# The down tiles' pair loads are issued from ScalarE's queue from the fifth expert on

## Chip, cores and metric

The kernel runs on one core of one Trainium2 chip. The metric is the device time of one execution in microseconds. Three runs of the kernel before give a median of 1706.59 us (1705.27 to 1707.78).

## The reference, cut to what matters

The program computes a two-layer transformer block and then a second block that ends in a mixture of experts. All weights are float32 and are read once. The change touches only the loads of the experts' weights:

```python
def expert_choice_ffn(h, w_router, w_gate, w_up, w_down):   # 16 experts
    cap = 2 * L // 16                                       # L = 272 tokens, cap = 34
    ...
    g, idx = lax.top_k(aff.T, cap)
    xg = hs[idx]                                            # 34 tokens of an expert
    a = jnp.einsum('ecd,edf->ecf', xg, w_gate)              # 1024 x 2048
    u = jnp.einsum('ecd,edf->ecf', xg, w_up)                # 1024 x 2048
    y = jnp.einsum('ecf,efd->ecd', jax.nn.silu(a) * u, w_down)   # 2048 x 1024
    ...
```

One expert needs 24 MB of weights (8 MB each for gate, up and down) and works on only 34 tokens.

## The kernel before

The kernel is one hand-written program for each engine, held together by semaphores. Weights come through a ring of six slots of 2 MB in SBUF (`RING_T`); the list `LOADS` fixes which tile goes into which slot and in which order. The experts' weights are cut into tiles of 2 MB: g0 to g3, u0 to u3 and d0 to d3 for each expert. From the fifth expert on (`PAIR_FROM = 4`, counting from zero) two neighbouring tiles make one pair of 4 MB that is loaded by one DMA into two neighbouring slots. An expert is then six pairs, in this order: G0, G1, G2, G3 (each gate tile with its up tile) and D0, D1 (d0 with d1, d2 with d3). Six slots are three pairs, so pair n goes where pair n-3 was: D0 of an expert follows G1 of the same expert, D1 follows G2, and G0, G1, G2 and G3 of the next expert follow G3, D0, D1 and that expert's own G0. The experts 4 to 14 are loaded this way whole; the last one, 15, has G0 to G2 as pairs and the rest in tiles and pieces.

SyncE issues every DMA (`sync_program`). For a pair, `pair_ring` (L3402 to L3408) waits at L3405 and L3406 until both slots have been left and issues the DMA at L3408. A slot is left when TensorE's last matmul that reads it is done: for a G pair this is the semaphore `u.full` of its PSUM bank, for a down tile `edown` or the bank of the expert's output.

TensorE (`pe_experts`) goes through an expert in this order: `gate_up(e, 0)`; in experts 3, 5, 7, 9, 11, 13 and 14 a `combine` of earlier outputs; `gate_up(e, 1)` to `gate_up(e, 3)`, each followed by the transposes of the hidden tile before it (`turn_hidden`, L1424); `down(e, 0)`; the gather of the next expert's tokens (`pick`, L1370); `down(e, 1)` to `down(e, 3)` with the transposes of `turn_picks` before the last. `gate_up` is the matmuls of L1412 and L1413, `down` those of L1439 and L1440.

ScalarE (`act_experts`) runs `gate(e, i)` for each gate tile: it waits for `u.full` of `gate_up(e, i)` and for VectorE's use of the buffer two tiles back, then one Silu (L2159). At the end of an expert it evicts two of the picks and one half of the output (L2184). VectorE multiplies (L3095), copies the transposed tiles and evicts the other half (L3136).

Of the kernel before, what the change touches and what calls it, by code (L numbers as in the profile page):

```python
# [24 lines left out]
E_N = 16  # L25
# [84 lines left out]
PAIR_FROM = 4  # L110
# [170 lines left out]
def flat(a):  # L281
    return a.rearrange("p a b -> p (a b)")
# [1239 lines left out]
def act_table(nc, n):  # L1522
    nc.scalar.add_instruction(mybir.InstLoadActFuncSet(
        name=nc.get_next_instruction_name(), engine=mybir.EngineType.Activation, act_func_set_id=n, ins=[], outs=[]))


def act_out(nc, u, dst, src, f=ACT.Copy, **kw):

    nc.scalar.wait_ge(u.full, u.n)
    nc.scalar.activation(dst, src, f, **kw).then_inc(u.taken, 1)  # L1530


def act_rms(nc, k, name, ps, n, a):

    i, s, u = RMS_AT[name], k.sem, k.banks["rms", name]
    nc.scalar.wait_ge(u.full, u.n)
    nc.scalar.activation(a, ps, ACT.Ln, bias=k.cc("eps"), scale=1.0 / n).then_inc(s["ln"], 1)
    nc.scalar.wait_ge(s["ln"], 2 * i + 1)
    nc.scalar.activation(a, a, ACT.Exp, scale=-0.5).then_inc(s["ln"], 1)
# [587 lines left out]
def act_experts(nc, k):  # L2127
    act, s, v, P = nc.scalar, k.sem, k.ex, k.banks
    act_out(nc, P["router"], v.LG, P["router"].t[:, 0:L])
    act_rms(nc, k, "ffn2", P["rms", "ffn2"].t[:, 0:3], D, v.RQ[:, 2, :])  # L2130
    u, roots = P["route"], v.RQ[:, 0, :]
    act.wait_ge(u.full, u.n)
    act.wait_ge(s["rscaled"], 1)
    for i, (r, m) in enumerate(TILES):
        act.activation(v.AFF[0:m, i, :], u.v(3, 16)[0:m, i, :], ACT.Exp, bias=v.mx[0:m, i:i + 1], scale=roots[0:m, i:i + 1],
                       accum_out=v.sm[0:m, i:i + 1]).then_inc(s["rexp"] if i < 2 else u.taken, 1)

    def turn_tokens(i):
        m = TILES[i][1]
        for half in range(2):  # L2140
            act_out(nc, P["tokens", i, half], v.FT[0:m, i, half * 512:half * 512 + 512], P["tokens", i, half].t[0:m, :],
                    scale=roots[0:m, i:i + 1])

    for i in range(3):
        turn_tokens(i)
    act_out(nc, P["affinity"], v.WK[0:16, 6:6 + L], P["affinity"].t[0:16, 0:L])

    def pick(e):
        for half in range(2):
            u = P["picks", e, half]  # L2150
            act_out(nc, u, v.XT[0:CAP, 256 * half:256 * half + 256], u.t[0:CAP, 0:256])

    def gate(e, i):
        u = P["egu", e, i]
        act.wait_ge(u.full, u.n)
        if 4 * e + i >= 2:
            t = P["egu", e, i - 2] if i >= 2 else P["egu", e - 1, i + 2]
            act.wait_ge(t.taken, t.done)
        act.activation(v.SG[:, i % 2, :], u.t[0:CAP, :], ACT.Silu).then_inc(s["esilu"], 1)  # L2159

    act_table(nc, SET_SILU)
    pick(0)
    for e in range(E_N):
        gate(e, 0)
        if 1 <= e <= 8:
            act_out(nc, P["back", e - 1], v.OGT[0:NP, e - 1, :], P["back", e - 1].t[0:NP, 0:L])
        for i in range(1, 4):
            gate(e, i)
        if e < E_N - 1:
            for q in range(4):  # L2170
                t = P["turned", e, q]
                act.wait_ge(t.full, t.n)
            pick(e + 1)
        else:
            act_table(nc, SET_EXP)

        u, g, r = P["eo", e], e // 2, 64 * (e % 2)
        act.wait_ge(u.full, u.n)
        if e == 0:
            act.wait_ge(s["yzero"], 1)  # L2180
        if g >= 2:
            t = P["comb", g - 2, KC - 1]
            act.wait_ge(t.full, t.n)
        act.activation(v.Y[r:r + CAP, g % 2, 0:512], u.t[0:CAP, :], ACT.Copy).then_inc(u.taken, 1)  # L2184

    def squares(i, half):
        u, n = P["fin", i, half], 2 * i + half
        act.wait_ge(u.full, u.n)
        act.activation(k.HWC[:, 512 * n:512 * n + 512], u.t[:, :], ACT.Square, accum_out=v.ss[:, i, half:half + 1]).then_inc(u.taken, 1)

    def root(i):
        a = v.fr[:, i, 1:2]
        act.wait_ge(s["fin_rs"], 5 * i + 1)
        act.activation(a, v.fr[:, i, 0:1], ACT.Ln, bias=k.cc("eps"), scale=1.0 / D).then_inc(s["fin_root"], 1)
        act.wait_ge(s["fin_root"], 2 * i + 1)
        act.activation(a, a, ACT.Exp, scale=-0.5).then_inc(s["fin_root"], 1)

    def final(i):
        x = v.XF[:, i, 512:1024]
        act.wait_ge(s["weighed"], 2 * i + 2)  # L2200
        act.wait_ge(s["fin_rs"], 5 * i + 5)
        act.activation(x, x, ACT.Identity, scale=v.fr[:, i, 3:4]).then_inc(s["final_a"], 1)

    squares(0, 0)
    squares(0, 1)
    squares(1, 0)
    root(0)
    squares(1, 1)
    root(1)
    final(0)  # L2210
    final(1)


def scalar_program(nc, k):
    high, split = [ActHigh(nc, k, layer) for layer in range(2)], ActSplit(nc, k)
    act_ab(nc, k, high[0])
    act_ffn(nc, k, 0, high[0], split)
    act_cd(nc, k, high[1])
    act_ffn(nc, k, 1, high[1], split)
    act_diff(nc, k, split)  # L2220
    act_experts(nc, k)
# [1073 lines left out]
def sync_program(nc, k):  # L3295
    sp, s, A, P = nc.sync, k.sem, k.A, k.banks
# [49 lines left out]
    u = P["rms", "mix1"]  # L3346
# [8 lines left out]
    def part(x, e, i):  # L3355

        if x == "d":
            return A["w_down_2"][e, i // 2][:, SLOT * (i % 2):SLOT * (i % 2 + 1)]
        return A["w_gate_up_2"][e, i][:, SLOT * (x == "u"):SLOT * (x == "u") + SLOT]
# [20 lines left out]
    u = P["rms", "ffn2"]  # L3380
# [15 lines left out]
    def beside_ring(x, e, i):  # L3396

        w = k.weight_at(x, e, i)
        sp.wait_ge(*w.prev.left)
        sp.dma_start(w.t, part(x, e, i)).then_inc(w.sem, 16)  # L3400

    def pair_ring(x, e, i):  # L3402

        head, tail = k.ring[x, e, i], k.ring[("u", e, i) if x == "g" else ("d", e, i + 1)]
        sp.wait_ge(*head.prev.left)  # L3405
        sp.wait_ge(*tail.prev.left)  # L3406
        src = A["w_gate_up_2"][e, i] if x == "g" else A["w_down_2"][e, i // 2]
        sp.dma_start(flat(k.ring.pair((x, e, i))), src).then_inc(head.sem, 16)  # L3408

    heads = set(PAIRED.values())  # L3410
    for e in range(E_N):
        if e:
            for i in range(4):
                for x in "gu":
                    if (x, e, i) in heads:
                        pair_ring(x, e, i)
                    elif (x, e, i) in PAIRED:
                        continue
                    elif (x, e, i) not in PIECES_OF and (x, e, i) != ("u", E_N - 1, 3):
                        beside_ring(x, e, i)  # L3420
        if e == 5:

            sp.wait_ge(*k.first["g", 3, 0].left)
            sp.dma_start(k.CB[:, :], A["fin"].broadcast_to([128, D])).then_inc(s["fin_in"], 16)
        if e == E_N - 1:


            w = k.ring["u", e, 3]
            sp.wait_ge(*w.prev.left)
            for c in range(2):  # L3430
                a, b = 2 * D * c, 2 * D * (c + 1)
                sp.dma_start(w.t[:, a:b], part("u", e, 3)[:, a:b]).then_inc(s[f"lastu{c}"], 16)
        for i in range(4):
            if ("d", e, i) in heads:
                pair_ring("d", e, i)
            elif e and (e < E_N - 1 or i < 2) and ("d", e, i) not in PIECES_OF and ("d", e, i) not in PAIRED:
                beside_ring("d", e, i)
    for i, n, first in ((2, 2, 0), (3, 4, 2)):
# [12 lines left out]
def build(nc, A, out):  # L3451
    k = Kit(nc, A, out)
    tensor_program(nc, k)
    scalar_program(nc, k)
    vector_program(nc, k)
    gpsimd_program(nc, k)
    sync_program(nc, k)
# [112 lines left out]
```

## Time and profile before

| | |
|---|---|
| median of three runs | 1706.59 us |
| the profiled execution, its own time | 1706.8 us |
| its span in the profile | 1704.9 us |
| TensorE busy | 1598.6 us, 94% |
| DMA bytes, mean rate over the span | 577.69 MB, 339 GB/s |
| pairs of 4 MB issued (G and D) | 47 and 22 |

How to read it: times in a trace are microseconds from the start of the span, and some 2 us of an execution lie outside it. TensorE (PE in the rows) is counted as busy while a matmul is in flight, even in stretches in which it waits for weights between tiles, so its 94% doesn't say that it is the bound. SPq is SyncE's own instruction stream, where a DMA shows only the time that issuing takes; the transfer itself shows as the time from issue to landing. A row "A <-B" with a time names who ended the idle time of A.

### The profile page before, as it was taken

What the parts mean: (1) busy time and instruction counts of PE and PEld (TensorE: products, weight loads), DVE (VectorE), ACT (ScalarE), POOL (GpSimd) and SP (SyncE); (2) the same over time, 40 slices, a digit from 0 to 9 for tenths busy, and PEclk for the clock granted to TensorE, in tenths of its full rate; (3) what the DMA queues carried; (4) which work ended last, traced back from release to release, by engine and by line L of the source; (5) the groups of instructions that cost most, each with busy time, mean ns of one, the idle gap of its engine ahead of it and who ended that gap; (6) DMA issues with size and microseconds to landing.
All of it is one profiled execution on the core that took longest, in us unless ns stands there. A gap on an engine that the chain in (4) does not pass through costs nothing.

```text
span 1704.9 us, 22910 instructions
## 1 busy us (share of the span) xinstructions
PE 1598.6 (94%) x9593; PEld 978.8 (57%) x9593; DVE 734.6 (43%) x1462; ACT 472.4 (28%) x839; POOL 34.3 (2%) x39
## 2 busy tenths in 40 slices
PE   7999999999999999999999989889889888888898
PEld 5787999998999999787322322323223223223332
DVE  3778889888886557895111111101101101011111
ACT  2526644448653437743000000000000000000001
POOL 0101000000000000100100000000000000000000
PEclk9999999999999999999999999999999999999999
DMA  9855478892466554249999999999999999999997
GB/s 388 354 244 216 170 314 343 324 353 84 173 254 223 190 195 176 100 155 391 402 429 430 431 435 433 432 433 431 431 433 433 434 431 431 431 434 432 431 430 297
DMA packets 36964, 577.69 MB, mean 339 GB/s; under 512 B 4192, under 2 KB 5248, under 8 KB 8192
## 3 DMA queue, kind: packets, MB, share of 16 engines
q1 hardware_dynamic: 36864, 576.24, 81.6%
q8 instruction: 77, 1.26, 0.3%
q14 instruction: 23, 0.19, 0.0%
HBM read 575.17 MB, written 1.05 MB: 338 GB/s over the span
## 4 chain that ended last, share of the span: by engine, by line
PE 70%; DMA 25%; DVE 2%; issue 2%; ACT 1%; SPq 0%; DVEq 0%; ACTq 0%
DMA RING_T<-in_w_gate_up 24%; PE P L1412 16%; PE P L1439 7%; PE P L986 5%; PE P L988 5%; PE P L987 5%; PE P L590 4%; PE P L1004 2%; PE P L1003 2%; PE P L1005 2%; PE P L599 2%; PE P L1370 1%; DMA RING_T<-in_w_down 1%; PE P L1174 1%; PE P L1176 1%
## 5 line engine op out<-in xcount | busy, mean ns | idle before, releaser
L1412 PE MATMUL P<-RING_T,SCR 128*34 128x512 f32 x928 | 421.5, 608 | 64.7 <-DMA RING_T<-in_w_gate_up 59.8
L1413 PE MATMUL P<-RING_T,SCR 128*34 128x512 f32 x960 | 436.7, 609 | 0.0
L1412 PEld LDWEIGHTS P<-RING_T,SCR 128*34 128x34 f32 x928 | 101.2, 114 | 332.3 <-issue 311.8
L3095 DVE TENSOR_TENSOR SCR<-P,SCR 34x512 f32<-34x512 f32 x64 | 44.4, 693 | 495.8 <-ACT SCR L2159 495.7
L1439 PE MATMUL P<-RING_T,SCR 128*34 128x512 f32 x480 | 220.6, 608 | 20.4 <-issue 19.6
L1440 PE MATMUL P<-RING_T,SCR 128*34 128x512 f32 x480 | 220.8, 609 | 0.0
L2159 ACT ACTIVATE SCR<-P 34x512 f32<-34x512 f32 x64 | 37.7, 589 | 538.1 <-PE P L1413 538.1
L986 PE MATMUL P<-SCF 128*128 128x256 f32 x640 | 181.1, 283 | 0.0
L988 PE MATMUL P<-SCF 128*128 128x256 f32 x640 | 181.1, 283 | 0.0
L987 PE MATMUL P<-SCF 128*128 128x256 f32 x640 | 181.1, 283 | 0.0
L1439 PEld LDWEIGHTS P<-RING_T,SCR 128*34 128x34 f32 x480 | 51.0, 114 | 153.5 <-issue 149.3
L986 PEld LDWEIGHTS P<-SCF 128*128 128x128 f32 x640 | 122.9, 192 | 0.0
L988 PEld LDWEIGHTS P<-SCF 128*128 128x128 f32 x640 | 122.9, 192 | 0.0
L987 PEld LDWEIGHTS P<-SCF 128*128 128x128 f32 x640 | 122.9, 192 | 0.0
L2644 DVE TENSOR_TENSOR SCF<-RING_T,SCF 128x1024 fp32r<-128x1024 f32 x88 | 106.1, 1220 | 30.0 <-ACT SCF L1808 30.0
L1808 ACT ACTIVATE SCF<-RING_T 128x1024 fp32r<-128x1024 f32 x88 | 91.9, 1053 | 52.7 <-PE P L1005 27.9
L1413 PEld LDWEIGHTS P<-RING_T,SCR 128*34 128x34 f32 x960 | 104.7, 114 | 0.0
L1530 ACT ACTIVATE SCR<-P 128x256 f32<-128x256 f32 (+7 forms) x112 | 45.1, 417 | 197.4 <-PE P L1370 122.8
L1003 PE MATMUL P<-SCF 128*128 128x256 f32 x352 | 99.6, 283 | 0.0
L1004 PE MATMUL P<-SCF 128*128 128x256 f32 x352 | 99.6, 283 | 0.0
L1005 PE MATMUL P<-SCF 128*128 128x256 f32 x352 | 99.6, 283 | 0.0
L2317 DVE SCALAR_TENSOR_TENSOR RING_T<-RING_T,CB 128x1024 f32<-128x1024 f32 x80 | 94.2, 1232 | 8.0 <-ACT CB L1623 4.1
(465 smaller groups left out, 2529.9 us busy)
## 6 DMA issues: line engine op xcount, KB each, us to landing
RING_T<-in_w_gate_up SPq DMA_DIRECT2D x47, 4096.0 KB, 20.7
RING_T<-in_w_down SPq DMA_DIRECT2D x22, 4096.0 KB, 21.7
RING_T<-in_ada_w SPq DMA_DIRECT2D x24, 2048.0 KB, 10.6
RING_T<-in_ffn_w SPq DMA_DIRECT2D x22, 2048.0 KB, 8.0
RING_T<-in_w_gate_up SPq DMA_DIRECT2D x17, 2048.0 KB, 16.8
RING_T<-in_ffn_w SPq DMA_DIRECT2D x22, 1024.0 KB, 6.6
RING_T<-in_w_down SPq DMA_DIRECT2D x11, 2048.0 KB, 17.6
RING_T<-in_ab_w_in SPq DMA_DIRECT2D x7, 2048.0 KB, 15.8
```

What stands on the lines that cost most here:

```text
L986: pe.matmul(o, wh, v.HH[:, 0, c, :], start=c == 0, stop=False)
L987: pe.matmul(o, wh, v.HH[:, 1, c, :], start=False, stop=False)
L988: ins = pe.matmul(o, wl, v.HH[:, 0, c, :], start=False, stop=c == KC - 1)
L1003: pe.matmul(o, wh, v.HR[:, f % NHD, 0, :], start=f == 0 and m % 2 == 0, stop=False, skip_group_check=True)
L1004: pe.matmul(o, wh, v.HR[:, f % NHD, 1, :], start=False, stop=False, skip_group_check=True)
L1005: ins = pe.matmul(o, wl, v.HR[:, f % NHD, 0, :], start=False, stop=f == 21, skip_group_check=True)
L1412: pe.matmul(u.t[0:CAP, :], xs, wg.v(KC, 512)[:, c, :], start=c == 0, stop=c == KC - 1)
L1413: ins = pe.matmul(u.t[64:64 + CAP, :], xs, wu.v(KC, 512)[:, c, :], start=c == 0, stop=c == KC - 1)
L1439: pe.matmul(u.t[0:CAP, :], hs, w.v(4, 1024)[:, c, 0:512], start=first, stop=end)
L1440: ins = pe.matmul(u.t[64:64 + CAP, :], hs, w.v(4, 1024)[:, c, 512:1024], start=first, stop=end)
L2317: nc.vector.scalar_tensor_tensor(out=src, in0=src, scalar=1.0, in1=k.CB[:, :], op0=ALU.mult, op1=ALU.mult, accum_out=k.MOD[:, layer, 4 * i ...
L2644: nc.vector.tensor_tensor(lo, w.up()[:, :, z, j * 128:(j + 1) * 128], hi.bitcast(F32), ALU.subtract).then_inc(k.sem["lo"], 1)
```

## The change

The DMAs that load D0 and D1 of experts 4 to 14 (22 DMAs of 4 MB) are taken out of SyncE's program and put into ScalarE's, behind `gate(e, 1)` and `gate(e, 2)`. Their waits, their sources, the slots that they fill and the semaphores that they raise stay the same. The G pairs, the last expert's loads and all else stay in SyncE's program in their order.

```diff
@@ act_experts @@
+    def load_downs(e, i):
+
+        head, tail = k.ring["d", e, i], k.ring["d", e, i + 1]
+        act.wait_ge(*head.prev.left)
+        act.wait_ge(*tail.prev.left)
+        act.dma_start(flat(k.ring.pair(("d", e, i))), k.A["w_down_2"][e, i // 2]).then_inc(head.sem, 16)
+
...
         for i in range(1, 4):
             gate(e, i)
+            if PAIR_FROM <= e < E_N - 1 and i < 3:
+                load_downs(e, 2 * (i - 1))
@@ sync_program @@
-    def pair_ring(x, e, i):
-
-        head, tail = k.ring[x, e, i], k.ring[("u", e, i) if x == "g" else ("d", e, i + 1)]
+    def pair_ring(e, i):
+
+        head, tail = k.ring["g", e, i], k.ring["u", e, i]
         sp.wait_ge(*head.prev.left)
         sp.wait_ge(*tail.prev.left)
-        src = A["w_gate_up_2"][e, i] if x == "g" else A["w_down_2"][e, i // 2]
-        sp.dma_start(flat(k.ring.pair((x, e, i))), src).then_inc(head.sem, 16)
+        sp.dma_start(flat(k.ring.pair(("g", e, i))), A["w_gate_up_2"][e, i]).then_inc(head.sem, 16)
...
             if ("d", e, i) in heads:
-                pair_ring("d", e, i)
+                continue
```

## Rows read from the trace of the kernel before

**Rows 1.** The page: DMA's share and rate in 40 slices; queues with packets, MB, share.

```profile
DMA  9855478892466554249999999999999999999997
GB/s 388 354 244 216 170 314 343 324 353 84 173 254 223 190 195 176 100 155 391 402 429 430 431 435 433 432 433 431 431 433 433 434 431 431 431 434 432 431 430 297
q1 hardware_dynamic: 36864, 576.24, 81.6%
```

**Rows 2.** Busy time by stretch: PE, PEld, DVE, ACT, POOL, then granted clock, DMA share, GB/s.

```profile
1416.50:1474.40 57.90, 52.57 (x258) 17.65 (x256) 9.11 (x23) 3.70 (x7) 0.00 (x0) 0.97 1.00 431
1474.40:1532.30 57.90, 48.71 (x242) 15.12 (x240) 6.15 (x15) 3.70 (x7) 0.00 (x0) 0.97 1.01 434
```

**Rows 3.** Waits from 1000 us on: engine, line, releaser, us in total, times, longest.

```profile
ACT SCR L2159 <- PE P L1413: 422.7, 48, 11.4
PE P L1412 <- DMA RING_T<-in_w_gate_up: 59.8, 35, 3.0
```

**Rows 4.** PE in order of time: four tiles' first matmuls, and the kernel's last weights.

```profile
1478.55 0.59 PE L1412 MATMUL P<-RING_T,SCR 128*34 128x512 f32 x1 [1.66 <-DMA RING_T<-in_w_gate_up]
...
1488.28 0.59 PE L1412 MATMUL P<-RING_T,SCR 128*34 128x512 f32 x1 [2.30 <-DMA RING_T<-in_w_gate_up]
...
1497.94 0.59 PE L1412 MATMUL P<-RING_T,SCR 128*34 128x512 f32 x1 [2.24 <-DMA RING_T<-in_w_gate_up]
...
1507.56 1.04 PE L1439 MATMUL P<-RING_T,SCR 128*34 128x512 f32 x1 [2.19 <-issue]
...
1693.21 0.62 PE L1439 MATMUL P<-RING_T,SCR 128*34 128x512 f32 x1 [0.16 <-DMA RING_T<-in_w_down]
```

**Rows 5.** SyncE in order of time: the six issues of expert 12, and the next.

```profile
1447.00 0.33 SPq L3408 DMA_DIRECT2D RING_T<-in_w_gate_up  x1
...
1461.76 0.33 SPq L3408 DMA_DIRECT2D RING_T<-in_w_gate_up  x1
...
1469.12 0.33 SPq L3408 DMA_DIRECT2D RING_T<-in_w_gate_up  x1
...
1476.98 0.33 SPq L3408 DMA_DIRECT2D RING_T<-in_w_gate_up  x1
...
1485.69 0.33 SPq L3408 DMA_DIRECT2D RING_T<-in_w_down  x1
...
1495.42 0.33 SPq L3408 DMA_DIRECT2D RING_T<-in_w_down  x1
...
1505.08 0.33 SPq L3408 DMA_DIRECT2D RING_T<-in_w_gate_up  x1
```

**Rows 6.** One issue of L3408 by itself: duration in ns, and its landing.

```profile
L3408 SPq DMA_DIRECT2D RING_T<-in_w_down x1: 328/328/328, 1485.7 to 1485.7; - x1
DMA to landing us min/median/max: 21.8/21.8/21.8
```

**Rows 7.** DMA issues of the whole kernel: count, KB each, median us to landing.

```profile
RING_T<-in_w_down SPq DMA_DIRECT2D x22, 4096.0 KB, 21.7
out<-SCR SPq DMA_DIRECT2D x4, 256.0 KB, 2.0
```

**Rows 8.** ACT in order of time: two Silus of expert 12.

```profile
1485.65 0.59 ACT L2159 ACTIVATE SCR<-P 34x512 f32<-34x512 f32 x1 [8.12 <-PE P L1413]
1495.38 0.59 ACT L2159 ACTIVATE SCR<-P 34x512 f32<-34x512 f32 x1 [9.14 <-PE P L1413]
```

**Rows 9.** PE in order of time: D0's start, the next G0's start, a combine.

```profile
1449.49 1.04 PE L1439 MATMUL P<-RING_T,SCR 128*34 128x512 f32 x1 [2.21 <-issue]
...
1469.83 0.62 PE L1412 MATMUL P<-RING_T,SCR 128*34 128x512 f32 x1 [0.80 <-DVE SCR L3136]
...
1534.86 3.94 PE L1455 MATMUL P<-SCR 98*128 98x272 f32 x16
```

**Rows 10.** The chain of waits: two loads from issue to landing; the instruction queue, 1300 to 1323.

```profile
1271.33 21.83 DMA RING_T<-in_w_gate_up
1300.55 22.34 DMA RING_T<-in_w_gate_up
...
q8 instruction: 1, 0.02, 0.2%
```

More of the change, by code:

```diff
@@ L3415, in sync_program @@
                     if (x, e, i) in heads:
-                        pair_ring(x, e, i)
+                        pair_ring(e, i)
                     elif (x, e, i) in PAIRED:
```

## The prediction

> **What bounds the kernel now.** I read the page's slices first. From the slice that starts at 853 us (20 x 42.6) the 16 DMA engines are busy all the time and move 429 to 435 GB/s, until the last slice [rows 1]; nearly everything goes through one queue, q1, which is SyncE's. Then busy time by stretch, in the part with pairs: DMA share 1.00 and 1.01, while TensorE's clock is at 0.97 and ScalarE is busy for 3.70 of 57.9 us [rows 2]. Then the waits: over the stage TensorE waits 59.8 us for gate and up weights in 35 waits, and ScalarE waits for TensorE [rows 3]. Then four tiles in order of time: each first matmul starts when its weights land, at 1478.55, 1488.28, 1497.94 and 1507.56, so a pair takes (1507.56 - 1478.55) / 3 = 9.67 us; the last wait is booked as "issue", but D0 was issued at 1485.69 and landed 21.8 us later, at 1507.5, so it is weights too [rows 4, 5, 6]. 4 MB in 9.67 us is 434 GB/s. An expert of six pairs is 58.0 us. The last matmuls still wait for weights at 1693.21 [rows 4]. So the end of the kernel is set by one stream of bytes that never pauses. What counts for a change is one thing: does it make that stream pause, or move faster.
>
> **What the queue looks like inside.** Of three pairs of slots one is being read by TensorE, one is on the wire, and one is queued. D0 is issued at 1485.69, when G1 has been read, and lands 21.8 us later; its own transfer is 9.67, so for 12.1 us it waits, behind 2.5 us of G2's rest and 9.67 of G3. G1's reading takes 1485.69 - 1478.55 = 7.1 us of the 9.67 [rows 4, 5, 6].
>
> **Part 1: 22 DMAs leave SyncE.** There are 22 [rows 7], at 0.33 us of issuing each [rows 5]. SyncE issues each G pair as soon as its slots are free and waits between (from 1485.69 to 1495.42 it has one thing to do) [rows 5], so this frees nothing: G0 to G3 wait for their own slots, which come free at the same times. 0 us.
>
> **Part 2: ScalarE issues them.** D0 goes behind gate(e, 1), which waits for the same matmul that leaves D0's slots, so the added waits pass at once. ScalarE's Silu of G1 starts at 1485.65, 0.04 us before SyncE's issue of D0, and takes 0.59 [rows 5, 8]. The issue is thus between 0 and 0.6 us later; I take 0.6. Queued behind it on ScalarE is gate(e, 2), 9.7 us away [rows 8], for which 0.33 us of issuing is nothing; VectorE and the transposes that wait for the Silu see no difference. That cover would be gone only if ScalarE were held at a wait, and none that the change adds can hold it. 0 us by itself, since the byte stream has 12.1 us of queue ahead of D0.
>
> **Part 3: two queues instead of one.** This is the only part with a price. In one queue D0 can't overtake G3. In two it can, and no row of this kernel shows two load queues at once. I take it that the engines serve both alike, since the small instruction packets of q8 get through while q1 is 20 us deep [rows 10]. Then the bytes in flight are the same, but G3 lands late. By hand for one expert, zero at G1's landing, steps of 9.67: G1 is read by 7.3, D0 is issued at 7.9. The shortest transfer in the trace lands 2.0 us after its issue, and its 256 KB are 0.6 of them, so 1.4 us pass until bytes flow [rows 7]: D0 moves from 9.3. G2 lands at about 9.9. Then G3 and D0 share, and both land near 29.0, where before G3 landed at 19.3 and D0 at 29.0. TensorE reads G2 until 17.2 (D1 is issued and queues behind D0), stands idle, and reads G3 from 29.1 to 36.3, or 37.9 if it restarts at half clock (D0's first matmul takes 1.04 us after a wait, others 0.59, some 1.6 us over the tile) [rows 4]. D1 has the wire alone from 29.0 and would land at 38.7. The next G0 is issued when G3 has been read, and its bytes come at 37.7 to 39.3: the stream pauses for 0 to 0.6 us. Then TensorE goes from G3 to D0 (1.0 us), and D0's slots come free 12.3 us after D0's start, 10.7 without the half clock (1449.49 to 1461.76) [rows 5, 9]: the next G1 is issued near 48.0 to 49.6, its bytes come at 49.4 to 51.0, and G0's bytes end at 48.4. A pause of 1.0 to 2.6 us. After that D1's slots are free 7.4 us later (1461.76 to 1469.12) [rows 5] and there is no further pause. Sum for the first expert with two queues: 1.0 to 3.2 us.
>
> The second expert is milder, because TensorE is now behind: it reads its G1 some 4 us later against the landing, so D0 is issued later, meets a G3 that is 3.6 us into its transfer, and G3 lands 6.1 us late, not 9.7. G0's bytes then come 4.7 us before the wire would run dry, and G1's 2.6 us before. In an expert with a combine (5, 7, 9, 11, 13, 14) another 3.94 us [rows 9] push D0's issue further back, and G3 is 2.1 us late. TensorE needs some 51 us for an expert without its waits (50.4 by the steps 7.1 x 4, three gaps of about 0.9 and 1469.83 - 1449.49 less 1.6), and 55 with a combine, of 58.0 [rows 4, 9]: it can make up what it lost. The other quiet experts (6, 8, 10, 12) come out between a pause of 0 and one like the first. I take 1.4 for the first, 0.2 for each of the four others, 0 for the six with a combine: +2.2 us. Bounds of this part: 0 (TensorE's lag always covers) and 5 x 3.2 = 16 (every quiet expert pays in full).
>
> **Sum.** The profiled execution took 1706.8 us, its span of 1704.9 and 1.9 around it: 1706.8 + 2.2 = 1709.0. It stands 0.2 above the median of the three runs, so I forecast 1708.8. The 11.7 us behind the last weights (1693.21 to 1704.9) [rows 4] stay as they are, since the last expert is in one queue again.
>
> **A rule of the skill.** The Trainium skill, "DMA: Bandwidth & Descriptors", section "Issuing engines are not separate DMA queues", says that DMAs of all issuers end on the same 16 engines and interleave, and that several issuers save only the issuing time; by it this change could gain nothing. The stream here is never short of issued work [rows 1, 2], which agrees. The same page, section "Queues, rings and completion order", says that an engine takes turns between queues and changes over only when a whole packet is done, where a packet is some 9 to 17 descriptors. By it an engine's share of a pair could be one packet, and the pairs would alternate whole; the time for that is rival 1.
>
> **Rival 1: whole pairs take turns.** D0 then goes on the wire as soon as G2 is done, at 9.7, and G3 behind it: D0 lands at 19.3, G3 at 29.0. G3 is as late as in the fair case, in each quiet expert, for a G3 that has already queued doesn't profit from TensorE's lag unless it has begun. For it: D0 is issued before G2 is done [rows 5, 6]. Against it: nothing in the rows. It pays about 0.6 us in each of the 11 experts, 1 us in the quiet ones: 6 to 8 us, 1714. Chance 0.17.
>
> **Rival 2: changing queues costs wire time.** The nearest rows: two loads in a row that land at 1293.16 and 1322.89, three steps apart, 29.73 and not 29.01 us, with one instruction packet of 16 KB between [rows 10]. At 27 GB/s an engine that packet is 0.6 us; 0.12 is over, for going there and back. If a pair is eight pieces per engine and each change costs 0.06 us, an expert with 16 to 30 changes loses 1 to 1.8 us: 11 to 20 us over 11 experts, 1722. It decides as soon as a change costs over 0.02 us. Chance 0.07.
>
> **Rival 3: one queue starves the other.** If ScalarE's queue always went first, D0 and D1 (issued at 17.8, before D0 is through) would both go ahead of G3: it lands at 38.7 with nothing left in flight, and the wire stands still until G3 is read and G0's bytes come, 7.2 + 0.1 + 1.4 = 8.7 us. Over 11 experts 96 us, some 1803. For it speaks only that no row shows the order; against it that q8 gets through. Chance 0.05.
>
> **Rival 4: the stream gets denser.** The best slice has 435 GB/s, the others of the stage 429 to 434, 432 in the mean [rows 1]. If a second queue fills the seams between DMAs and all slices come to 435, 0.7% of some 620 us are gained: 4.3 us, 1702.3. For it: the room exists. Against: the queue is never empty, and the pair's step of 9.67 is already 434. Chance 0.09.
>
> **Rival 5: the change does nothing.** If the engines kept the order of issue, all would stay at 1706.6. Chance 0.10.
>
> **How the numbers follow.** The fair case has 0.52. A measurement of this kernel can tell about 0.2% from no change, 3.4 us. The fair case lies within that for most of its range and reaches past it with about 0.05; rival 5 lies within; rival 1 is past it, with about 0.03 within. Faster 0.09 (rival 4); same 0.52 - 0.05 + 0.10 + 0.03 = 0.60; slower 0.05 + 0.14 + 0.07 + 0.05 = 0.31. The range of 1703.5 to 1719 leaves out most of rival 4, the upper half of rival 2 and rival 3, some 0.17.
>
> **What would show it.** DMA share in the stretches stays 1.00 and the rate 431 to 434; q1 splits, with 22 x 4 MB (92 MB) in a second queue. D0's time to landing stays near 21, or gets shorter, G3's grows from about 21 to 25 to 30 us. TensorE's waits for G3 get longer (3.0 is the longest now) and those for D0 and G0 go away; the sum of its waits stays. Rate under 425 in the stage would speak for rival 2; stretches with DMA share under 0.9 once per expert for rival 3. I am wrong if the stage gets shorter, or if pauses add up to more than 3 us.

## The result, and the profile after

The changed kernel took 1721.6 us, 1719.0 and 1723.9 us in three executions; a fourth took 4088 us and is left out (with it the median is 1722.74). Against 1706.57 us before, the ratio is 1.009, with an interval of 1.0076 to 1.0104: 15 us slower. I had forecast 1708.8 us and a range up to 1719.0. The profiled execution took 1721.58 us, its span grew from 1704.9 to 1719.6, by 14.7 us.

The page of the kernel after: rate in 40 slices, queues (packets, MB, share of 16 engines), and the issues of pairs (count, KB, median us to landing).

```profile
GB/s 390 355 245 202 185 305 363 320 346 56 208 237 241 151 241 146 126 172 377 406 430 430 434 432 397 427 424 429 426 417 417 428 414 425 432 403 436 429 431 305
q1 hardware_dynamic: 33696, 483.96, 68.9%
q10 hardware_dynamic: 3168, 92.28, 12.5%
RING_T<-in_w_gate_up SPq DMA_DIRECT2D x47, 4096.0 KB, 16.6
RING_T<-in_w_down ACTq DMA_DIRECT2D x22, 4096.0 KB, 21.4
```

The 22 DMAs moved as the diff says: 92 MB now go through q10. The stage that ran at 429 to 435 GB/s [rows 1] has slices of 397, 403, 414 and 417. The next fence is busy time by stretch of the kernel after (us, PE, PEld, DVE, ACT and POOL busy, granted clock, DMA share, GB/s): one stretch in which two pairs share the wire, then the pauses: two behind the late G3 of expert 4, one behind the late D1 of expert 5 (1127 to 1133), one in expert 6 (1177 to 1183), and two each behind the late G3 of the experts 8, 10 and 12.

```profile
1264.00:1280.00 16.00, 6.98 (x32) 2.37 (x30) 0.99 (x2) 0.59 (x1) 0.00 (x0) 0.71 1.02 440
...
1045.00:1051.00 6.00, 6.00 (x34) 1.77 (x32) 0.99 (x2) 0.59 (x1) 0.00 (x0) 1.00 0.68 240
1057.00:1063.00 6.00, 6.00 (x36) 1.78 (x34) 0.27 (x2) 0.00 (x0) 0.00 (x0) 1.00 0.91 344
1127.00:1133.00 6.00, 5.20 (x26) 1.32 (x24) 0.69 (x1) 0.59 (x1) 0.00 (x0) 1.00 1.01 399
1177.00:1183.00 6.00, 6.00 (x38) 1.73 (x34) 0.64 (x4) 0.00 (x0) 0.00 (x0) 1.00 0.93 377
1286.00:1292.00 6.00, 6.00 (x34) 1.83 (x30) 0.99 (x2) 0.59 (x1) 0.00 (x0) 1.00 0.71 268
1298.00:1304.00 6.00, 6.00 (x36) 1.78 (x34) 0.64 (x4) 0.00 (x0) 0.00 (x0) 1.00 0.91 350
1405.00:1411.00 6.00, 6.00 (x32) 1.69 (x28) 0.99 (x2) 0.59 (x1) 0.00 (x0) 1.00 0.77 279
1417.00:1423.00 6.00, 6.00 (x36) 1.72 (x34) 0.64 (x4) 0.00 (x0) 0.00 (x0) 1.00 0.92 350
1525.00:1531.00 6.00, 6.00 (x35) 1.82 (x32) 0.99 (x2) 0.59 (x1) 0.00 (x0) 1.00 0.84 317
1536.00:1542.00 6.00, 6.00 (x36) 1.78 (x34) 0.63 (x4) 0.00 (x0) 0.00 (x0) 1.00 0.91 350
```

While both queues are served the rate is 440 GB/s, not less than with one (435 in the same stretch before). The loss is in pauses. Against 432 GB/s, 6 us at 268 are 6 x (1 - 268/432) = 2.3 us, at 350 another 1.1: expert 8 pays 3.4 us. By the same sum expert 4 pays 3.9, expert 10 3.3, expert 12 2.7, expert 6 0.8, and expert 5, which has a combine, 0.5: 14.5 us, where the span grew by 14.7. The landings of G1 say the same of the experts without a combine: from their G1 to the next expert's pass 62.0, 59.5, 60.9, 61.8 and 61.2 us, where before they were 58.1 to 58.2, together 14.6 us more. That these sums meet the 14.7 to 0.2 us is partly chance: the executions of the changed kernel lie 4.9 us apart, and in the trace of before the same stretch takes 59.5 us in the experts 9 and 13, which in the change have 58.0 and 58.1.

One expert in detail, expert 8. Its gate and up pairs on SyncE and its down pairs on ScalarE, in order of time (start, duration), and the first matmul of G3:

```profile
1251.33 0.33 SPq L3416 DMA_DIRECT2D RING_T<-in_w_gate_up  x1
...
1258.79 0.59 ACT L2159 ACTIVATE SCR<-P 34x512 f32<-34x512 f32 x1 [6.48 <-PE P L1413]
1258.85 0.33 ACTq L2166 DMA_DIRECT2D RING_T<-in_w_down  x1
...
1279.37 1.04 PE L1412 MATMUL P<-RING_T,SCR 128*34 128x512 f32 x1 [9.02 <-DMA RING_T<-in_w_gate_up]
...
1287.93 0.33 SPq L3416 DMA_DIRECT2D RING_T<-in_w_gate_up  x1
...
1298.87 0.33 SPq L3416 DMA_DIRECT2D RING_T<-in_w_gate_up  x1
```

The times to landing of four of these issues by themselves: G3 (issued at 1251.33), D0 (1258.85), D1 (1270.08), the next G0 (1287.93).

```profile
DMA to landing us min/median/max: 27.9/27.9/27.9
...
DMA to landing us min/median/max: 21.6/21.6/21.6
...
DMA to landing us min/median/max: 20.6/20.6/20.6
...
DMA to landing us min/median/max: 12.4/12.4/12.4
```

G3 lands at 1279.2 and D0 at 1280.5, together: they shared the wire. The two queues by themselves, from 1264 to 1274 (packets, MB, share of 16 engines), and the stretch in which TensorE starts on G3:

```profile
q10 hardware_dynamic: 70, 2.29, 53.1%
q1 hardware_dynamic: 71, 2.13, 49.3%
...
1279.30:1281.30 2.00, 1.94 (x6) 0.66 (x8) 0.00 (x0) 0.00 (x0) 0.00 (x0) 0.50 0.95 410
```

ScalarE's queue (q10) and SyncE's (q1) move about the same. TensorE stood idle for 9.0 us ahead of G3 and started it at a granted clock of 0.50, the lower of its two levels (1.2 of 2.4 GHz), with 1.04 us a matmul, not 0.59. It released G3 at 1287.9; D1 lands at 1290.7, and the next G0, issued on a wire about to run dry, takes 12.4 us, where its bytes need 9.67. ScalarE is innocent of lateness: its issue stands 0.06 us behind the start of its Silu.

### The profile page after: what moved, and what is told of

Read it like the earlier page. It is cut to its first block, busy times and chain, and to the rows that moved or that the text cites. A ratio compares the mean times of both kernels' runs of the same rounds, so it can differ in the third digit from the quotient of the medians.

```text
span 1719.6 us, 22910 instructions
## 1 busy us (share of the span) xinstructions
PE 1603.2 (93%) x9593; PEld 970.5 (56%) x9593; DVE 735.3 (43%) x1462; ACT 472.9 (27%) x839; POOL 34.3 (2%) x39
## 3 DMA queue, kind: packets, MB, share of 16 engines
q10 hardware_dynamic: 3168, 92.28, 12.5%
## 4 chain that ended last, share of the span: by engine, by line
PE 78%; DMA 17%; DVE 2%; ACT 1%; issue 1%; SPq 0%; DVEq 0%; ACTq 0%
PE P L1412 19%; DMA RING_T<-in_w_gate_up 13%; PE P L1439 11%; PE P L986 4%; PE P L988 4%; PE P L987 4%; DMA RING_T<-in_w_down 4%; PE P L590 4%; PE P L1004 2%; PE P L1003 2%; PE P L1005 2%; PE P L1370 2%; PE P L599 2%; PE P L1174 1%; PE P L1175 1%; PE P L1176 1%
## 6 DMA issues: line engine op xcount, KB each, us to landing
RING_T<-in_w_gate_up SPq DMA_DIRECT2D x17, 2048.0 KB, 14.8
```

## Experiments

Theory P at the start: the pauses behind an overtaken G3 are the whole loss, and only experts without a combine have them. Rival S: a second queue costs wire time by itself. Rival L: ScalarE issues late.

### Half of the experts

```diff
+ON_ACT = (4, 6, 8, 10, 12)            # second kernel: (5, 7, 9, 11, 13, 14)
-            if PAIR_FROM <= e < E_N - 1 and i < 3:
+            if e in ON_ACT and i < 3:
```

> The down pairs of experts 4, 6, 8, 10 and 12 alone (those without a combine) are issued from ScalarE's queue, the others stay in SyncE's. Theory P (pauses): D0 overtakes G3, and the stream runs dry twice behind a late G3, only in experts without a combine, where each costs 3.1 us. The whole loss of the change, 15 to 16 us, is then here: 1721 to 1724 us. Rival S (a second queue costs wire time whenever it is in use, 16 us over 11 experts, 1.45 each): 5 x 1.45 = 7 us, 1714 us.

> The down pairs of experts 5, 7, 9, 11, 13 and 14 alone (those with a combine) are issued from ScalarE's queue. Theory P: D0 is issued some 4 us later against the stream there, G3 is already on the wire, and nothing runs dry: 0 to 3 us, 1707 to 1710 us (expert 14 follows another with a combine and has the least certain place). Rival S: 6 x 1.45 = 9 us, 1715 us.

Measured, as the ratio to the kernel before with its interval: 1.0087 (1.0069 to 1.0106), 14.8 us, for the experts without a combine; 1.0067 (1.0043 to 1.0092), 11.4 us, for the others. The first is what P said. The second fits neither. The two halves together lose 26 us where the whole change loses 15, so the cost isn't one per use of the queue, which speaks against S, and it isn't tied to the missing combine either, which speaks against P: an expert with a combine is spared in the full change only because of what the expert before it has left behind. The traces bear this out: in expert 9 D0 is issued 12.7 us after G1's landing in the change and 8.6 us when only the experts with a combine are changed, and G3 then takes 28.9 us to land, not 21.2.

### Later issues

```diff
-            if PAIR_FROM <= e < E_N - 1 and i < 3:
-                load_downs(e, 2 * (i - 1))
+            if PAIR_FROM <= e < E_N - 1 and i > 1:      # one tile later
+                load_downs(e, 2 * (i - 2))
...
+                for _ in range(5):                      # other kernel: 3 us of dependent copies ahead of load_downs
+                    ...
+                    act.activation(v.LG[:, 0:256], k.C[:, 0:256], ACT.Copy).then_inc(s["delay"], 1)
```

> As the change, but D0 is issued behind gate(e, 2) and D1 behind gate(e, 3), one gate tile later each. Theory P: D0's bytes come some 19 us after G1's landing, when G3 is through or nearly so, so nothing overtakes: 1706 to 1709 us, though both queues are in use. Rival S: unchanged, 22 pairs still use the second queue, 1720 to 1724 us.

> As the change, but five dependent copies on ScalarE, about 3 us together, stand ahead of each of the 22 issues. Theory P: G3 has 3 us more on the wire before D0 joins, lands 3 us earlier, and the pauses of 2 and 1 us in a quiet expert are mostly covered: 1707 to 1711 us; issuing later makes it faster. Rival L (the loss comes from ScalarE issuing late or being held up): slower than the change, 1724 us or more. Rival S: as the change, 1720 to 1724 us.

Measured: 1.0576 (1.0551 to 1.06), 98 us slower, and 1.0143 (1.0121 to 1.0165), 24 us slower. P falls as I had put it. The second time, 1732 us, is what rival L forecast (1724 or more), so L is left to the next experiment. The trace of the later issues shows what I had left out: D1 and the next expert's G0, issued at the same moment, and their times to landing.

```profile
1238.55 0.33 SPq L3416 DMA_DIRECT2D RING_T<-in_w_gate_up  x1
1238.56 0.36 ACTq L2166 DMA_DIRECT2D RING_T<-in_w_down  x1
...
DMA to landing us min/median/max: 25.4/25.4/25.4
...
DMA to landing us min/median/max: 23.0/23.0/23.0
```

The first landing is D1's, the second G0's. TensorE needs D1 before G0, but they share the wire all the way, and D1 comes last. Two of this kernel's dry stretches:

```profile
1202.00:1208.00 6.00, 5.21 (x26) 1.30 (x24) 0.69 (x1) 0.59 (x1) 0.00 (x0) 1.00 0.56 193
1225.00:1234.00 9.00, 9.00 (x48) 2.53 (x45) 1.39 (x4) 0.59 (x1) 0.00 (x0) 1.00 0.22 65
```

So there can be two crossings in an expert, D0 with G3 and D1 with the next G0, and a later issue relieves the first and feeds the second. Theory Q, from here on: what costs is any pair that shares the wire with one that TensorE needs earlier.

### One queue again, but ScalarE's

```diff
+        load_gates(e, 3)               # behind gate(e, 0)
...
+        load_gates(e + 1, 0)           # behind gate(e, 3)
+            load_gates(e + 1, 1)       # behind pick(e + 1)
+        load_gates(e + 1, 2)           # behind the eviction of the expert's output
-                        pair_ring(e, i)
+                        if e == PAIR_FROM:
+                            pair_ring(e, i)
```

> From expert 5's G0 on every pair, G and D, is issued from ScalarE's queue in the old order, so the stream is in one queue again (only around experts 4 and 15 both are in use). Theory Q (order): what costs is that with two queues a pair shares the wire with one that TensorE needs earlier (D0 with G3, the next G0 with D1). In one queue none does: 1706 to 1711 us. Rival A (ScalarE as the issuer costs: late issues, a slower queue): 1722 us or more, with 67 issues instead of 22.

Measured: 1.0032 (1.0021 to 1.0043), 5.5 us slower, a median of 1711.57 us, just past Q's figure. Two stretches of it, the border at expert 4, where its D0 is in one queue and its G3 in the other, and 520 us of the stage:

```profile
1045.00:1062.00 17.00, 17.00 (x97) 5.02 (x94) 2.15 (x5) 1.34 (x3) 0.00 (x0) 1.00 0.94 371
1070.00:1590.00 520.00, 457.62 (x2244) 151.45 (x2242) 71.04 (x175) 34.91 (x67) 0.00 (x0) 0.97 1.00 433
```

17 x (1 - 371/432) = 2.4 us are lost at this crossing; then 433 GB/s for the rest of the stage, against 423 in the change. ScalarE issues 65 pairs here and the stage loses no rate by it, so L is out. The rest of the 5.5 us lies at the other border, in expert 15, whose G2 comes from ScalarE's queue and the tiles behind it from SyncE's: G2 takes 24.7 us to land, where before it took 20.5, TensorE waits 4.5 us for it, and the span ends 16.5 us behind the last weights, not 11.7.

### One of the two pairs

```diff
-            if PAIR_FROM <= e < E_N - 1 and i < 3:
+            if PAIR_FROM <= e < E_N - 1 and i == 1:     # D0 alone; other kernel: i == 2, D1 alone
```

> As the change, but only D0 is issued from ScalarE's queue; D1 goes back to SyncE's, behind G3 and ahead of the next G0. Theory Q: D0 still halves G3's rate, so G3 is 8 to 9 us late and the stream runs dry behind it; D1 is no longer halved by the next G0, so TensorE loses its lag and every expert pays: 1718 to 1724 us. Rival S (wire time for each use of the second queue): 11 uses instead of 22, 1714 us.

> As the change, but only D1 is issued from ScalarE's queue; D0 goes back to SyncE's. Theory Q: D1 halves the rate of D0, which TensorE needs first and whose slots the next G1 needs; D0 lands up to 8 us late, and TensorE's reading of D0 to its release takes 10.7 us, longer than G3's 7.1, so the pause is longer than in the change: 1726 to 1738 us. Rival S: 11 uses instead of 22, 1714 us.

Measured: 1.0148 (1.0133 to 1.0164), 25 us, for D0 alone, and 1.0279 (1.0264 to 1.0295), 48 us, for D1 alone. Half of the change costs more than all of it, which S can't give; both lie past Q's figures too (1731.9 and 1754.4 us), in its direction, so Q's sizes by hand are no more than rough. With D0 alone, D1 stands behind G3 in SyncE's queue and shares the wire with D0, which the change spares it: D0 of expert 8 takes 24.4 us to land, 21.6 in the change. In the kernel with D1 alone, D0 (in SyncE's queue) now takes 24.9 us to land and D1 23.6, and the wire runs dry while TensorE reads D0 to its release. Its pairs' issues and one such stretch:

```profile
RING_T<-in_w_down SPq DMA_DIRECT2D x11, 4096.0 KB, 24.9
RING_T<-in_w_down ACTq DMA_DIRECT2D x11, 4096.0 KB, 23.6
...
1308.00:1316.00 8.00, 8.00 (x46) 2.34 (x44) 0.85 (x2) 0.76 (x2) 0.00 (x0) 1.00 0.44 156
```

### One crossing

```diff
+ON_ACT = (8,)
```

> Only expert 8's two down pairs are issued from ScalarE's queue, all else as in the kernel before. Theory Q: G3 of expert 8 lands some 9 us late, the stream runs dry twice behind it, 3 us together, and from expert 9 or 10 on pairs land in steps of 9.67 us again with nothing given back: 1709 to 1710.5 us. If what was lost could be made up later, 1706 to 1707 us.

Measured: 1.002 (1.001 to 1.0029), 3.4 us slower, 3.0 by the medians (1709.29 us). Its two pauses, and the 290 us behind them:

```profile
1278.00:1284.00 6.00, 6.00 (x32) 1.84 (x30) 0.99 (x2) 0.59 (x1) 0.00 (x0) 1.00 0.67 246
1292.00:1298.00 6.00, 6.00 (x36) 1.78 (x34) 0.64 (x4) 0.00 (x0) 0.00 (x0) 1.00 0.92 350
...
1300.00:1590.00 290.00, 254.20 (x1256) 83.73 (x1256) 40.33 (x100) 19.10 (x36) 0.00 (x0) 0.98 1.00 432
```

6 x (1 - 246/432) + 6 x (1 - 350/432) = 2.6 + 1.1 = 3.7 us lost, then 432 GB/s as before: the stream is as fast as it was, so nothing is given back. This run also shows how long TensorE's lag lasts. In expert 9 D0 is issued 12.5 us after G1's landing, in expert 10 again 7.3 us, as before the change, and TensorE stands waiting for G1 of expert 10:

```profile
1364.56 0.59 PE L1413 MATMUL P<-RING_T,SCR 128*34 128x512 f32 x1 [2.49 <-DMA RING_T<-in_w_gate_up]
```

The lag is gone within one expert, though nothing overtakes anything behind expert 8.

### Both queues, in the order of need

```diff
-        sp.dma_start(flat(k.ring.pair(("g", e, i))), A["w_gate_up_2"][e, i]).then_inc(head.sem, 16)
+        sp.dma_start(flat(...)[0:64, :], A["w_gate_up_2"][e, i][0:64, :]).then_inc(head.sem, 16)     # and 64:128 from ScalarE
...
+        sp.dma_start(flat(...)[:, 0:SLOT], A["w_gate_up_2"][e, i][:, 0:SLOT]).then_inc(head.sem, 16) # other kernel: by tiles, and SLOT:2 * SLOT from ScalarE
```

> From expert 4's D0 on every pair is loaded as two DMAs of 64 partitions, one from SyncE's queue and one from ScalarE's, at the same places and in the old order, so both queues are in use all the time and both hold the pairs in the order in which TensorE needs them. Theory Q (order alone costs): no pair shares the wire with one needed earlier: 1706 to 1710 us. Rival S (two queues on one engine cost wire time): at least as slow as the change, 1722 us or more, since they share for the whole stage.

> As the run with both queues in order, but a pair is split by its tiles, not by partitions: the first tile of each pair (128 partitions, 16 KB each) comes from SyncE's queue and the second from ScalarE's, issued at the same places. Theory Q (order alone costs): both queues in use all the time, in the order of need: 1706 to 1710 us. Rival S (two queues cost wire time): 1722 us or more.

Measured: 1.3241 (1.3194 to 1.3287) for halves by partitions, 1.0038 (1.0023 to 1.0053), 6.5 us, for halves by tiles, whose 1713.27 us lie 3.3 past Q's figure and far below S's. The first doesn't speak of queues. Its stretches: expert 4's gate and up pairs, halves too, but all in SyncE's queue; then a stretch with both queues.

```profile
992.00:1020.00 28.00, 13.26 (x59) 3.80 (x59) 1.60 (x6) 1.46 (x3) 0.00 (x0) 0.76 0.98 208
...
1400.00:1500.00 100.00, 57.59 (x225) 16.12 (x227) 5.16 (x13) 3.50 (x7) 0.00 (x0) 0.78 1.00 244
```

With one queue the DMAs of 64 partitions make 208 GB/s, with two 244: the rate is low already with one queue, so the split by partitions is the cause, and with both queues it is rather higher. The kernel split by tiles has whole partitions:

```profile
1043.00:1060.00 17.00, 17.00 (x102) 5.22 (x100) 2.21 (x6) 1.34 (x3) 0.00 (x0) 1.00 0.90 354
...
1070.00:1590.00 520.00, 450.74 (x2228) 149.52 (x2224) 71.02 (x175) 34.91 (x67) 0.00 (x0) 0.98 1.01 429
```

The second row: 429 against 432 GB/s are 3.6 us over 520. The first is the border of expert 4, where half of D0 still overtakes G3: 17 x (1 - 354/432) = 3.1 us. Together, 6.7, they cover its 6.5. Both queues in use for the whole stage cost at most those 3.6 us, and rows of 16 KB in place of 32 may be part of that; it isn't separated. S is dead as the cause of the 15.

### TensorE's clock and TensorE's lag

```diff
+        if i == 3 and e in QUIET:                # 32 idle matmuls ahead of G3's wait; another kernel: 18
+            pe_busy(nc, k, u, 32)
...
+        if i == 1 and e in QUIET:                # 15 ahead of gate_up(e, 1); another kernel: 9
+            pe_busy(nc, k, u, 15)
```

> As the change, with 32 idle matmuls of 128x256 (some 8 us) ahead of the wait for G3's weights in the experts 4, 6, 8, 10 and 12, where TensorE stands idle for some 10 us and reads G3 at half clock at first (8.7 us, not 7.1). Theory C (the half clock is part of the price): G3 is released 1.6 us earlier, the first pause of an expert is 1.6 us shorter and the second too: 5 x 1.6 = 8 us off, some 1714 us. If the half clock plays no part, or the gap left before G3 is still long enough for it: 1720 to 1724 us.

> The filler ahead of G3 in the experts 4, 6, 8, 10 and 12 with 18 idle matmuls, 7.9 us at the 0.44 us that one was seen to take; the wait there is 9.3 us in the change. Theory C (the half clock behind the wait is part of the price): G3 is read in 7.1 to 7.5 us, not 8.7, and its release, the next G0 and so the end of both pauses come 1.2 to 1.6 us earlier: 1714 to 1717 us. If the clock plays no part: 1720 to 1724 us.

> As the change, with 15 idle matmuls of 128x256 (some 3.9 us, as much as a combine) ahead of gate_up(e, 1) in the experts 4, 6, 8, 10 and 12, which have no combine. Theory Q: TensorE reads G1 later there, D0 joins later, G3 has more of its transfer behind it, and TensorE's lag carries on from expert to expert, so more work on TensorE makes the kernel faster than the change: 1708 to 1717 us. Rival T (the loss is TensorE's time): 5 x 3.9 more, 1735 us or more.

> As the change, with 9 idle matmuls (4.0 us) ahead of gate_up(e, 1) in the experts 4, 6, 8, 10 and 12, the size of a combine, where 15 were 6.6 us. Theory Q by hand: D0 is issued some 2 us later against G1's landing, G3 lands 2 us earlier, and of the 3 us of pauses 2 are covered in each: 1709 to 1715 us. If every shift of TensorE only moves the loss from G3 to D1, as the 15 matmuls did: 1719 to 1724 us.

I had mis-sized the filler at first: 32 took 14.08 us, 0.44 each (the trace counts two rows for each), and overran the wait.

```profile
1273.88 14.08 PE L581 MATMUL P<-C 128*128 128x256 f32 x64
```

That kernel has 1.0167 (1.0150 to 1.0184), 28 us: a G3 released later makes the pause longer, as Q says, but nothing of the clock. With 18 the ratio is 1.0070 (1.0053 to 1.0086), 12 us, against 15 for the change: 1718.96 us, between C's figure and the other, with intervals that overlap. It isn't a clean test either. In the experts 6 and 8 the filler still ran when G3 had landed and held it up by 4.2 and 2.7 us. In expert 4 it ended 2.7 us ahead of G3, which was read in 9.0 us at 0.81 all the same. In 10 and 12 it did what it should: G3 is read in 7.3 us at a granted clock of 1.00, where the change takes 9.0 and 8.8 at 0.80 and 0.82. From G1 to the next G1 it is then 60.3 and 61.1 us, where the change has 61.8 and 61.2, so the two differ by 1.5 and 0.1 us. What the lower clock costs over the stage stays open.

With 15 matmuls ahead of G1 (6.7 us each time) the ratio is 1.0083 (1.0066 to 1.0100), as the change: 1721.5 us, 4.5 past Q's figure and far below T's, with 34 us more of TensorE's work for nothing lost and nothing won. With 9 (4.1 us) it is 1.0043 (1.0028 to 1.0059), 7.3 us, with 1715.55 us at the end of Q's figure: half of the loss is gone with 20 us more work on TensorE. Time on TensorE isn't what is short. That the lag shifts both crossings, with a best place between G3's and D1's, is how I read these two runs; no more places were tried.

No version tried beats the kernel before; its single queue in the order of need already fills the wire.

## Why the prediction was wrong

**What bounds the kernel**: right. The stream of bytes sets the end, its rate fell from 432 to 423 GB/s over 1070 to 1590 us, and the pauses sum to the loss.

**Parts 1 and 2**: right as far as the runs show. ScalarE's issue was 0.06 us behind its Silu's start (I had taken 0.6), and with 65 issues from it the stage kept its rate (433 GB/s). SyncE's relief wasn't tried by itself; the pauses leave nothing for it.

**Part 3, the first expert**: right in kind and nearly in size. By expert 8, from G1's landing (1251.4): D0 issued at 7.5 (I had 7.9), G3 landed at 27.8 (29.0), D0 at 29.1 (29.0), D1 at 39.3 (38.7), next G0 issued at 36.5 (36.3 to 37.9), next G1 at 47.5 (48.0 to 49.6). The pauses were 2.3 and 1.1 us where I had 0 to 0.6 and 1.0 to 2.6. The first was too small because I took 1.4 us from issue to bytes, from a transfer of 256 KB; the next G0 and G1, issued as the wire ran dry, landed 12.4 and 13.4 us after their issue, 2.7 and 3.7 over their 9.67. My 3.2 us for the top of this range also counts 0.6 twice: if G0's bytes start 0.6 us late, they end at 49.0, not 48.4, and the second pause is 2.0, the sum 2.6. The measured 3.4 lies above that.

**The step that failed** is the one after: "I take 1.4 for the first, 0.2 for each of the four others". Measured: 3.9 for expert 4, and 0.8, 3.4, 3.3 and 2.7 for 6, 8, 10 and 12, with 0.5 for expert 5, together 14.5 where I had 2.2. I let TensorE's lag cover the experts behind the first. It does cover the next one: in expert 9 D0 was issued at 1324.97, 12.7 us after G1's landing at 1312.3, and nothing ran dry. But it is used up there. In the experts 8, 10 and 12 D0 was issued 7.5, 8.0 and 7.3 us after G1's landing, in step with the stream as in expert 4 (7.3), and each paid again nearly as expert 4 did; only in expert 6 some lag was left (11.1 us), and it paid 0.8. The reason stood in my own text: TensorE needs 51 us of the 58 (its terms add up to 49.8, not the 50.4 that I wrote), so it makes up some 7 us in an expert without a combine. I read that as a comfort and not as the end of the cover. The kernel with one crossing shows it by itself: its lag is gone in expert 10, though no second crossing follows.

There is a second thing that I had wrong: that D1 has the wire alone. The next G0, whose slot G3 left early, joins it. D1 of expert 9 took 23.5 us to land and TensorE waited for it:

```profile
1355.83 0.62 PE L1439 MATMUL P<-RING_T,SCR 128*34 128x512 f32 x1 [2.45 <-DMA RING_T<-in_w_down]
```

In the change the pauses above leave little for this second crossing, 0.5 us behind the late D1 of expert 5. The later issues (98 us) show what it can cost.

**The bound held and the value did not.** I had written an upper bound of 5 x 3.2 = 16 for exactly this case, and the measured 15 lies at it. Part of that is luck: without the 0.6 counted twice the bound is 13, and the five experts paid 0.8 to 3.9, not 3.2 each. I should have noticed that the range's end, 1719, left most of it out, and that "TensorE's lag always covers" was argued for one expert and used for five. The combine was mis-sized as well: it stands between G0 and G1, and with TensorE in step it delays D0 by about 2 us, not 3.94. Before the change D0 is issued 8.6 to 10.0 us after G1's landing in the experts with a combine and 7.2 to 7.3 in those without. That fits the 11.4 us that the experts with a combine pay when they are the only ones changed.

**The rivals.** Rival 1 (whole pairs take turns): no; from 1264 to 1274 both queues moved over 2 MB, D0 and G3 landed 1.3 us apart, and D0 didn't land first. Its time, 1714, was nearer than mine, for the wrong reason. The rule of the Trainium skill (DMA: Bandwidth & Descriptors, Queues, rings and completion order), that an engine changes queues only after a whole packet, isn't contradicted by this, but a packet in its sense can't have been a pair's whole share on an engine. Rival 2 (changing queues costs wire time) had almost the measured time, 1722, and is refuted by 440 GB/s in the shared stretch and by half of the change costing more than the whole. Rivals 3, 4 and 5 didn't come. My own sign of being wrong, pauses of over 3 us together, did.

## What to carry to other kernels

When one stream of loads fills the wire, look at the order in which its bytes arrive, not at who issues them: here a second queue let a later load take half the rate of the one that was needed next, and the ring of three pairs ran dry behind it. Split over two queues that both held it in the order of need, the same stream lost at most 3.6 us in 520. A pause on a full stream wasn't given back in the 290 us that followed. And before a cost that was worked out for one iteration is called covered in the later ones, the engine's slack has to be carried through two full periods: slack that makes up a lag also ends its cover.

## What the runs showed of the hardware

- Two queues of the same 16 engines are served about equally and at full rate: 2.13 and 2.29 MB in 10 us, and 440 GB/s in a stretch shared by G3 and D0, which land 1.3 us apart.
- A DMA onto 64 partitions runs at about half rate: 208 GB/s in one queue, 244 with the other 64 partitions in a second queue, where whole-partition loads make 432.
- A 4 MB load issued as the wire runs dry landed 12.4 us after its issue (13.4 the one behind it), where its bytes need 9.67; a 256 KB store took 2.0 us in all [rows 7].
- TensorE's granted clock was 0.50 for the first 2 us behind an idle wait of 9.0 us, and a tile's reading took 8.8 to 9.0 us instead of 7.3; with filler matmuls in the wait, up to 1.0 us before its end, it was 1.00.
- The costs of parts of this change don't add: 14.8 and 11.4 us for its two halves by expert, 25 and 48 us for its two halves by pair, 15 us for the whole.
